# Two transformer blocks in float32 on one core: weights 64 bytes off the period, and three 256-column products in a row for a 512 and a 256 one

## What is computed

```python
# first block
z = rmsnorm(x) @ w_in                       # 2048 x 5200
x = x + concat(y_pool, y_attn) @ w_out      # 2048 x 2048
up = rmsnorm(x) @ w_up                      # 2048 x 11264
c = conv_b + sum(conv_w[j] * shifted(up, j) for j in range(3))
x = x + (silu(gate) * val) @ w_down         # 5632 x 2048
# second block
mod = silu(c) @ w_mod + b_mod               # 2048 x 12288, one row
z = (rmsnorm(x) * (1 + sc) + sh) @ w_in_2   # 2048 x 6160
x = x + g_m * rmsnorm(concat(y_conv, y_gla) @ w_out_2)
x = x + g_f * rmsnorm(conv_ffn_2(...))      # w_up_2, w_down_2
```

## Time and profile before

| | |
|---|---|
| median of 3 executions | 2218.85 us (2218.2 to 2219.58) |
| the profiled execution | 2217.98 us |
| its span, first to last instruction | 2215.9 us |
| granted TensorE clock, mean | 0.999 of full speed |
| PE busy | 2206.9 us (100%), 11916 matmuls |
| DVE busy | 1624.4 us (73%) |
| ACT busy | 1154.8 us (52%) |
| DMA | 233 GB/s over the span |

### The profile page before, as it was taken

The page is one execution under the profiler, slowest core; times in us unless marked ns, Lnnn a source line. Parts: engine busy times, 40 slices in busy tenths (PEclk is TensorE's granted clock), DMA queues, the critical chain, the costliest instruction groups (busy, mean ns, idle before and its releaser), DMA issues.

```text
span 2215.9 us, 31578 instructions
## 1 busy us (share of the span) xinstructions
PE 2206.9 (100%) x11916; PEld 1912.6 (86%) x11916; DVE 1624.4 (73%) x1917; ACT 1154.8 (52%) x1466; POOL 69.2 (3%) x47
## 2 busy tenths in 40 slices
PE   9999999999999999999999999999999999999999
PEld 9888888888888888888898888888888888888887
DVE  8789677888888877667766767787887666675555
ACT  6454546554555554444646555465555455554444
POOL 0005200000000000000000200000000000000000
PEclk9999999999999999999999999999999999999999
DMA  8767476577777866878575556766877655555553
GB/s 324 282 208 243 139 285 228 190 283 286 278 285 283 287 233 235 299 272 310 191 254 187 168 171 190 266 218 238 294 275 248 226 190 189 189 181 200 196 197 118
DMA packets 208136, 517.24 MB, mean 233 GB/s; under 512 B 12320, under 2 KB 46624, under 8 KB 183856
## 3 DMA queue, kind: packets, MB, share of 16 engines
q1 hardware_dynamic: 203200, 513.38, 65.9%
q10 hardware_dynamic: 4848, 2.65, 0.4%
HBM read 513.88 MB, written 2.11 MB: 233 GB/s over the span
## 4 chain that ended last, share of the span: by engine, by line
PE 95%; DVE 3%; ACT 1%; DMA 0%; SPq 0%; issue 0%; ACTq 0%; DVEq 0%
PE ps L2134 29%; PE ps L2143 15%; PE ps L2044 14%; PE ps L2046 14%; PE ps L2045 14%; PE ps L2164 4%; PE ps L2173 2%; DVE w_lo L1191 1%; DVE raw L1211 0%; DMA raw<-in_w_in 0%; PE ps L2578 0%; PE ps L2434 0%; PE ps L2360 0%; PE ps L2357 0%; PE ps L2354 0%; PE ps L2494 0%
## 5 line engine op out<-in xcount | busy, mean ns | idle before, releaser
L1191 DVE TENSOR_TENSOR w_lo<-raw,w_hi 128x1024 fp32r<-128x1024 f32 x757 | 937.6, 1248 | 534.2 <-ACT w_hi L575 533.4
L575 ACT ACTIVATE w_hi<-raw 128x1024 fp32r<-128x1024 f32 x757 | 789.7, 1057 | 905.9 <-PE ps L2046 350.9
L2134 PE MATMUL ps<-a_hl,w_hi 128*128 128x512 f32 x2684 | 625.7, 390 | 0.0
L2134 PEld LDWEIGHTS ps<-a_hl,w_hi 128*128 128x128 f32 x2684 | 498.2, 188 | 99.7
L2044 PE MATMUL ps<-w_hi,a_hl 128*128 128x512 f32 x1216 | 475.4, 391 | 0.0
L2046 PE MATMUL ps<-w_hi,a_hl 128*128 128x512 f32 x1216 | 473.3, 389 | 0.0
L2045 PE MATMUL ps<-w_lo,a_hl 128*128 128x512 f32 x1216 | 473.2, 389 | 0.0
L2143 PEld LDWEIGHTS ps<-a_hl,w_lo 128*128 128x128 f32 x2688 | 333.9, 192 | 6.7
L2143 PE MATMUL ps<-a_hl,w_lo 128*128 128x256 f32 x2688 | 336.2, 283 | 0.0
L2044 PEld LDWEIGHTS ps<-w_hi,a_hl 128*128 128x128 f32 x1216 | 228.3, 188 | 47.7 <-issue 0.7
L2046 PEld LDWEIGHTS ps<-w_hi,a_hl 128*128 128x128 f32 x1216 | 228.3, 188 | 47.4
(11 more groups left out here) (269 smaller groups left out, 1394.5 us busy)
## 6 DMA issues: line engine op xcount, KB each, us to landing
raw<-in_w_up SPq DMA_DIRECT2D x176, 1024.0 KB, 4.9
raw<-in_w_mod SPq DMA_DIRECT2D x96, 1024.0 KB, 5.2
raw<-in_w_down SPq DMA_DIRECT2D x88, 1024.0 KB, 4.9
raw<-in_w_in SPq DMA_DIRECT2D x86, 1024.0 KB, 5.2
raw<-in_w_out SPq DMA_DIRECT2D x32, 1024.0 KB, 6.2
x<-in_x SPq DMA_DIRECT2D x2, 1024.0 KB, 8.0
region<-gate_rows ACTq DMA_DIRECT2D x2, 1024.0 KB, 7.2
out_x<-x SPq DMA_DIRECT2D x8, 256.0 KB, 2.2
```

The lines of the kernel that those rows point to most:

```text
L575: nc.scalar.activation(hi_of(hh), raw[:, n % RAW_SLOTS, half * HALF:(half + 1) * HALF], ACT.Copy).then_inc(hi_ready, 1)
L1191: v.tensor_tensor(lo_of(hh), raw[:, n % RAW_SLOTS, half * HALF:(half + 1) * HALF], hi_of(hh).bitcast(F32), ALU.subtract).then_inc(lo_ready, 1)
L2134: mm = mmul(dst[:, BLOCK * ft:BLOCK * (ft + 1)], hi_of(hh, columns(kk, ft)), a[:, kts[kk], :, :].rearrange("p l s -> p (l s)"), start=firs ...
```

## The change

Two things are done. The halves of layouts M and S and of the W pair of in2 (with in2's narrow rest) lie 16 elements (64 bytes) further in their slots of `w_hi` and `w_lo`; for that both tensors get 64 elements more, and a half that follows a shifted one and is not shifted itself lies 64 elements (256 bytes) further until slot 0 comes round. A slot whose data reaches into the next one may be written only when that next one's earlier half is used too: `slot_used_by` then names a half one later, which is so for 14 halves, all in the first four of a run in which the offset grows. The area `region` is 160 elements shorter, and one window in it is moved. Second, `parts_apart` takes the place of the 512-and-256 order: tile by tile, w_hi against hi, w_hi against lo, w_lo against hi, 256 columns each, half by half. The first blocks of up1 and up2 (`half_M`) keep their order, and the first blocks' first eight halves their place. The instructions of ACT, DVE and SP are the same in number and order.

```diff
 def slot_used_by(hh):
-    return hh - 2 * HL_SLOTS if hh - HL_SLOTS in APART else hh - HL_SLOTS
+    own = hh - 2 * HL_SLOTS if hh - HL_SLOTS in APART else hh - HL_SLOTS
+    after = hh - 3 - HL_SLOTS if hh - 3 in APART else hh - 3
+    into_next = hh % HL_SLOTS < HL_SLOTS - 1 and OFFSET[hh] > OFFSET[after]
+    return max(own, after) if into_next else own
...
+def slot_offsets():
+    shifted = {2 * PH["in2"].rest + n for n in range(2)}
+    for name in RUNS:
+        for a, b, layout in RUNS[name]:
+            for i in range(a, b):
+                first = 2 * PH[name].pairs[i].m0
+                if layout == "S" or (layout, name) == ("W", "in2"):
+                    shifted.update(range(first, first + 16))
+                elif layout == "M":
+                    shifted.update(range(first + (8 if i == 0 else 0), first + 16))
+    offsets = []
+    for hh in range(2 * len(RAW_OF) + 4):
+        if hh in shifted:
+            offsets.append(OFF_LINE)
+        else:
+            offsets.append(NEXT_PERIOD if hh % HL_SLOTS and offsets[hh - 1] and hh - 1 not in APART else 0)
+    return offsets
...
-        w_hi = sb("w_hi", [P, HL_SLOTS, HALF], F32R)
-        w_lo = sb("w_lo", [P, HL_SLOTS, HALF], F32R)
+        w_hi = sb("w_hi", [P, HL_SLOTS * HALF + NEXT_PERIOD], F32R)
+        w_lo = sb("w_lo", [P, HL_SLOTS * HALF + NEXT_PERIOD], F32R)
...
-            return w_hi[:, hh % HL_SLOTS, cols]
+            at = HALF * (hh % HL_SLOTS) + OFFSET[hh]
+            return w_hi[:, at + cols.start:at + cols.stop]
...
-            def chunk_in_runs(c, parts):
-                (rounded0, remaining0), (rounded1, remaining1) = parts
-                if c % 2 == 0:
-                    rounded0()
-                    rounded1()
-                    remaining0().then_inc(w_used, 1)
-                    remaining1().then_inc(w_used, 1)
-                else:
-                    remaining0()
-                    remaining1()
-                    rounded0().then_inc(w_used, 1)
-                    rounded1().then_inc(w_used, 1)
+            def parts_apart(dst, hh, kts, width, first, last, r=0, a=a_hl):
+                pe.wait_ge(lo_ready, hh + 1 + 16 * r)
+                for kk, kt in enumerate(kts):
+                    for ft in range(width // P):
+                        wc = slice(kk * width + ft * P, kk * width + (ft + 1) * P)
+                        main_part, low_part = dst[:, BLOCK * ft:BLOCK * ft + S], dst[:, BLOCK * ft + S:BLOCK * (ft + 1)]
+                        end = last and kk == len(kts) - 1
+                        mmul(main_part, hi_of(hh, wc), a[:, kt, 0, :], start=first and kk == 0, stop=end, skip_group_check=True)
+                        mmul(low_part, hi_of(hh, wc), a[:, kt, 1, :], start=False, stop=False, skip_group_check=True)
+                        mm = mmul(low_part, lo_of(hh, wc), a[:, kt, 0, :], start=False, stop=end, skip_group_check=True)
+                return mm
```

More of the change, by code:

```diff
@@ L56 @@
 OFF_LINE = 16
+NEXT_PERIOD = 64
 BLOCK_CHUNKS = KT // KC
@@ L162 @@
 APART.update({2 * (PH["out2"].pairs[1].m0 + 6) + n: (0, 2048, 8192, 10240)[n] for n in range(4)})
+RUNS = {
+    "in1": [(0, 1, "W"), (1, 2, "T"), (2, 3, "T"), (3, 4, "S"), (4, 5, "T")],
+    "out1": [(0, 1, "T"), (1, 2, "T")],
+    "up1": [(0, 1, "M"), (1, 2, "M"), (2, 3, "M"), (3, 10, "M"), (10, 11, "M")],
+    "in2": [(0, 1, "W"), (1, 2, "T"), (2, 3, "T"), (3, 4, "S"), (4, 5, "S"), (5, 6, "S")],
+    "out2": [(0, 1, "T"), (1, 2, "T")],
+    "up2": [(0, 1, "M"), (1, 2, "M"), (2, 5, "M"), (5, 6, "M"), (6, 11, "M")],
+}
+def slot_offsets():
[15 more added lines that the diff above has]
+    return offsets
+OFFSET = slot_offsets()
 def slot_used_by(hh):
-    return hh - 2 * HL_SLOTS if hh - HL_SLOTS in APART else hh - HL_SLOTS
+    own = hh - 2 * HL_SLOTS if hh - HL_SLOTS in APART else hh - HL_SLOTS
+    after = hh - 3 - HL_SLOTS if hh - 3 in APART else hh - 3
+    into_next = hh % HL_SLOTS < HL_SLOTS - 1 and OFFSET[hh] > OFFSET[after]
+    return max(own, after) if into_next else own
 def raw_stride(pair):
@@ L227, in lo_of @@
                 return region_r[:, APART[hh] + HALF + cols.start:APART[hh] + HALF + cols.stop]
-            return w_lo[:, hh % HL_SLOTS, cols]
+            at = HALF * (hh % HL_SLOTS) + OFFSET[hh]
+            return w_lo[:, at + cols.start:at + cols.stop]
         def main(g):
@@ L367, in two_blocks @@
         act_ready = sem("act_ready")
[L370 to L377, removed]
         K_ORDER = {name: (0, 1, 2, 3) for name in RUNS}
@@ L1198, in rest_lows @@
                     dve.wait_ge(hi_ready, hh + 1)
-                    v.tensor_tensor(w_lo[:, hh % HL_SLOTS, 0:n_el], REST[name][:, half * n_el:(half + 1) * n_el],
-                                    w_hi[:, hh % HL_SLOTS, 0:n_el].bitcast(F32), ALU.subtract).then_inc(lo_ready, 1)
+                    v.tensor_tensor(lo_of(hh, slice(0, n_el)), REST[name][:, half * n_el:(half + 1) * n_el],
+                                    hi_of(hh, slice(0, n_el)).bitcast(F32), ALU.subtract).then_inc(lo_ready, 1)
             def lead(name, halves=range(4)):
@@ L1483, in fill_first @@
                     part = slice(BLOCK * kk, BLOCK * (kk + 1))
-                    v.tensor_tensor(w_lo[:, h, part], raw[:, h // 2, BLOCK * (kt % 4):BLOCK * (kt % 4 + 1)], w_hi[:, h, part].bitcast(F32),
+                    v.tensor_tensor(lo_of(h, part), raw[:, h // 2, BLOCK * (kt % 4):BLOCK * (kt % 4 + 1)], hi_of(h, part).bitcast(F32),
                                     ALU.subtract).then_inc(lo_ready if kk else sem("w_tile_low"), 1)
@@ L2094, in half_W, with first_tile, half_M @@
                 return mm
-            def first_tile(dst, a, slot, weights_low, low):
+            def first_tile(dst, a, hh, weights_low, low):
                 def four(weights, l, start=False):
                     for ft in range(4):
-                        mmul(dst[:, ft * S:(ft + 1) * S], weights[:, slot, ft * P:(ft + 1) * P], a[:, 0, l, :], start=start and ft % 2 == 0,
+                        mmul(dst[:, ft * S:(ft + 1) * S], weights(hh, slice(ft * P, (ft + 1) * P)), a[:, 0, l, :], start=start and ft % 2 == 0,
                              stop=False, skip_group_check=True)
-                four(w_hi, 0, True)
+                four(hi_of, 0, True)
                 pe.wait_ge(*weights_low)
-                four(w_lo, 0)
+                four(lo_of, 0)
                 pe.wait_ge(*low)
-                four(w_hi, 1)
-            def half_M(dst, hh, kts, first, last, r, a=a_hl, bank_free=None, pair_done=None, halves_apart=False):
+                four(hi_of, 1)
+            def half_M(dst, hh, kts, first, last, r, a=a_hl, bank_free=None, pair_done=None):
                 def columns(kk, ft):
@@ L2153, in half_M @@
                 return rounded()
[L2155 to L2177, removed]
@@ L2242, in body @@
                                     pe.wait_ge(epi_done, b)
-                                parts = []
+                                if name == "up1" and i0 == 1 and blk == 0:
+                                    pe.wait_ge(act_ready, 8 * (f + i0) + 2 * c + 2)
                                 for half in range(2):
@@ L2246, in body @@
                                         kts = [2 * KC * (c % 2) + KC * half + kk for kk in range(KC)]
[L2247 to L2255, removed]
+                                        mm = parts_apart(main(c // 2), hh + half, kts, S, c % 2 + half == 0, c % 2 + half == 2)
+                                    else:
+                                        kts = [KC * K_ORDER[name][c] + 2 * half + kk for kk in range(2)]
+                                        early = name == "up1" and i0 == 0
+                                        mm = parts_apart(quad(blk), hh + half, kts, BLOCK, c + half == 0, c == BLOCK_CHUNKS - 1 and half == 1, r,
+                                                         a_raw_up if early else a_hl)
+                                    mm.then_inc(w_used, 1)
                                 if between:
```

18 lines of the change are left out of this document (7 added, 11 removed).

## The result

The changed kernel takes 2235.6 us (median of 6, 2235.07 to 2236.97) where the one before, in the same runs, took 2218.33. The ratio is 1.0078, with an interval of 1.0065 to 1.0091: 17 us slower, not 26 faster.

What follows compares the result with a forecast made beforehand. PE's instruction stream was taken as the bound; -19.6 (M), -3.7 (S) and -2.5 (W in in2) sum to -25.8 us against 2217.98, so 2192.2, forecast as a median of 2193 us, range 2188 to 2206.

Steps and rivals of the forecast that it cites:

- What bounds the kernel: Whole span: PE busy throughout at 2.4 GHz, so time goes only where its stream shortens or a new wait arises.
- rival 1: M and S: toll paid per product wherever weights lie, 360 ns a tile, +40.6 us, 2259 us; 6%.
- the first of the sum: M in up1 and up2: 2688 tiles fall from 347.3 to 340.0 ns each, -19.6 us.
- S: Four pairs of 128 tiles, 512 tiles at the same price as M's: -3.7 us.
- W in in2: Order kept, weights shifted: 124 tiles fall from 360 to 340 ns, -2.5 us.
- The new wait: A half needs its remainder at its first tile; 8.2 us of lead against 6.7 us of work: cost zero.
- the later slots: `slot_used_by` one half later for 14 halves, 8.2 us of lead in place of 10.9: zero to 1 us each, taken as zero.
- DMA and DVE: DMA in up1 from 283 to 289 GB/s, nothing; DVE's queue follows the halves, attention work keeps its place, cost zero.
- Rival 3: Remainders come too late in up1 and up2, two halves 0.25 us late per pair: +10 us, 2203 us; 8%.
- rival 2's second case: Only one of a tile's three products freed: 353.3 ns a tile, +19.2 - 0.8 us, 2237 us; 2%.
- the shift would do nothing: Weight shift: consequence drawn from the skill's independent read ports; the trace's 113.3 against 120 ns was held to disagree.
- The columns plus 2.5 ns: Skill's matmul price: one more product costs 2.5 ns a tile, 8 us in all, near 2227 us; part of 6%.

Runs made afterwards that it cites:

- experiment 2: Changed kernel with the weight shift removed, keeping three products of 256 columns in a row in M and S: 2259.35 us.
- experiment 8: Changed kernel plus one extra product of 208 columns in each of up1 and up2, ahead of the second pair's first half: 2202.73 us.
- experiment 7: Changed kernel plus an extra product of 16 to 240 columns ahead of each half in 9 of 11 pairs of up1 and up2: 2256.88 us.
- experiment 1: Changed kernel with weights still shifted, but M and S back in the earlier order of 512 and 256 columns in runs: 2216.45 us.
- experiment 9: Earlier order of 512 and 256 columns in runs; in M and S only w_lo shifted by 64 bytes, w_hi on the period: 2211.04 us.

## Why the prediction was wrong

- **What bounds the kernel** was right: PE's stream, at the full clock, before and after. The prices of before, 227.5, 119.7, 347.3 and 360 ns, stood; experiment 2 gave 2259.35 us where rival 1 had 2259 for three products at 120.
- **The step that failed** is the first of the sum, "I take in1's 340, since that is the same sequence at the same distance". The tile cost 353.3. The same sequence at the same distance has two prices, and in1 showed one of them. It could have shown the other: with 192 bytes, where in1 is as before, in1's first stretch ran at 353.3. Its records from 10 to 16 us there:

```profile
L2074 PE MATMUL ps<-region_r,w_hi 128*128 128x256 f32 x18 | 5.1, 281 | 0.0
```

  2688 tiles of M by 13.3 ns are 35.8 us of the error of 42.6; S is 5 more, and the rest in2's W, restarts and waits.
- That the price of 340 was there to be had in M is shown by experiment 8, 2202.73 us: nothing that the forecast looked at told which of the two the changed kernel would fall into (all six executions took 2235 to 2237 us), and it did not know that there were two. The 10 us from there to the forecast are S and the first blocks, still at 353.3 for the most part, and restarts.
- S: about 370 of its tiles I counted at 353.3 and about 117 at 340. In place of -3.7 us it gave about +1.4.
- W in in2: -1.6 us in place of -2.5. With its narrow rest it took 50.74 us where it had taken 52.34; a stretch of six tiles ran at 353.3, and each interruption costs a restart. The shift-only kernel gained 2.1 us in all.
- The new wait, the later slots, DMA and DVE: at zero, rightly, but for 0.7 us of waits in S; in M not one, as the lead of 8.2 us against 6.7 said. Rival 3 did not occur.
- **The rivals.** The time, 2235.6 us, is that of rival 2's second case, one product in three freed, 353.3 ns and 2237 us, to which I gave 2%. Its numbers were right and its reason not: no fixed one of the three products is freed, all three start 117.4 to 118.3 ns apart, and the same three run at 340 elsewhere. Rival 1 (no toll lowered at all) was wrong in M too: without the shift it would be 24 us more.
- The Trainium skill, page "TensorE: Matmul & The Clock Gate", section "Step-by-step: what each phase is for", has it that loading weights takes no read bandwidth from a running matmul. Whether bandwidth is what is lost, no run here can show, but the place of the weights alone does move the price of a product, by some 6 ns either way (119.7 to 113.4, 227.5 to 233.1), so "the shift would do nothing" was no safe reading of it.
- The columns plus 2.5 ns of the Trainium skill, same page, section "Back-to-back issue gap", are given for a matmul in isolation, and the page says itself that they under-count beside loads where a product is narrow. They do here: one product more per tile cost 12.7 ns in experiment 2, not 2.5.
- What the trace of before could tell: the W pair of in1 has three stretches with interruptions between them, all at 340, but they are one pair and one layout of one execution, and I put 80% on them. Rigid prices gave no warning: the 120 ns on the period are as rigid and have no second state.

## What to carry to other kernels

A price read from starts holds for the stretch it was read in. Where products and weight loads start side by side, as here, look for a second stretch with the same code before you multiply by thousands of tiles, and make one if there is none. Where a long stretch runs at the dearer of two steady prices, one small product at its head may be worth more than any reordering; try it and read the starts behind it, since the width doesn't tell which state follows. And test the two halves of a change apart: here the split cost 41 us and the shift gave back 24, and the shift by itself 2.

## What the runs showed of the hardware

- The toll of a product with a weight load beside it depends on where the two operands lie to each other, with a period of 128 bytes: 2259.35 us at 0, 2243.22 at 32, 2235.6 at 64, 2259.43 at 128, 2237.53 at 192. Each is the time in the state that M happened to take; at 64 bytes it can be 2202.73 (experiment 8). No run shifts both operands alike, so that it is their distance and not the place of either is argued, from in1 (activations shifted) and in2 (weights shifted) having one price, 340.
- On the period a 256-column product with a full weight load costs 120 ns in every stretch. 64 bytes off it there are two steady states, 340.0 and 353.3 ns per three, kept for up to 1344 tiles and changed only by a disturbance.
- The code does not fix the state: behind the same interruption the last S stretch of in1 ran at 340 in the changed kernel (from 191.0 us) and at 353.3 in experiment 8 (from 190.9 us), whose instructions up to there are the same; the interrupted tile took 0.935 us in the one and 0.954 in the other.
- A product of 16 to 240 columns with a load of 128 columns costs about what one of 256 does (experiment 7).
- A 512-column product behaves the other way: 227.5 ns on the period, 233.1 off it, as far as experiment 1 shows. Shifting w_lo alone leaves it at 227.5 (experiment 9).
- Left open: what differs inside the chip between the two states, and why a stretch behind in1's or S's interruptions falls into either. The loads' records are no sure sign: in the changed kernel one in three is 192 ns long in the dearer state and none in the cheaper, but with 192 bytes M has none in the dearer state either. Whether S and the first pairs can be brought to 340 too wasn't tried. The kernel of experiment 8, 2202.73 us, is the fastest one here, faster than both.
